# Delta rule's scan: lengths of queries and keys kept as columns, gate sums from two matmuls, decays by subtraction

## The reference, cut to what matters

```python
q_a = l2norm(to_chunks(cq, GDN_HEADS)) * (GDN_HEAD_DIM ** -0.5)
k_a = l2norm(to_chunks(ck, GDN_HEADS))        # x * rsqrt(sum(x*x) + 1e-6)
g_a = -exp(gdn_a_log) * softplus(ga + gdn_dt_bias)
beta_a = sigmoid(gb)

gc = cumsum(g, axis=-1)                                        # inside a chunk
decay = exp(where(incl, gc[..., :, None] - gc[..., None, :], -inf))
kk = einsum('bhnid,bhnjd->bhnij', k, k)
lower = where(strict, beta[..., :, None] * kk * decay, 0.0)
rhs = concatenate([beta[..., None] * v, (beta * exp(gc))[..., None] * k], -1)
sol = triangular_solve(lower, rhs, unit_diagonal=True)         # -> u, w
a_qk = einsum('bhnid,bhnjd->bhnij', q, k) * decay
# for every chunk, in order, with the state S of each head:
delta = u - w @ S
o     = (q * exp(gc)) @ S + a_qk @ delta
S     = exp(gc[-1]) * S + (k * exp(gc[-1] - gc)).T @ delta
# then
o_a = rmsnorm(o, gdn_norm_g) * silu(gz)       # eps 1e-6 inside the mean
```

## Time and profile before

| | |
|---|---|
| median of three runs | 2850.66 us |
| the profiled execution's own time | 2850.46 us |
| its span, first to last instruction | 2849.1 us |
| PE matmul busy | 2665.6 us, 94% |
| DVE busy | 1396.9 us, 49% |
| ACT busy | 913.2 us, 32% |
| POOL busy | 172.9 us, 6% |
| granted TensorE clock, mean | 0.967 of full speed |

### The profile page before, as it was taken

How to read it: one execution, slowest core, us unless ns; L and a number is a source line. 1 busy time by engine, 2 the same in 40 slices (tenths; PEclk the granted TensorE clock), 3 DMA queues, 4 the chain that set the end, 5 groups by cost and what they waited for, 6 DMA issues and landing times.

```text
span 2849.1 us, 34291 instructions
## 1 busy us (share of the span) xinstructions
PE 2665.6 (94%) x15010; PEld 2231.9 (78%) x15010; DVE 1396.9 (49%) x1632; ACT 913.2 (32%) x1254; POOL 172.9 (6%) x185
## 2 busy tenths in 40 slices
PE   6988989989998999999988999889999999999998
PEld 4866778878887877787877987678888878788886
DVE  5664453444365436565355337556553354433333
ACT  4332223244334443122233237532122232322222
POOL 0001230000001000000012100010000100100001
PEclk9998999999999999999999999999999999999999
DMA  3210000221132314454222200035542223232221
GB/s 115 84 64 31 16 17 31 90 75 69 64 133 96 127 59 171 154 207 155 97 82 74 75 30 1 1 135 210 206 158 90 93 85 104 74 104 90 102 94 69
DMA packets 39302, 265.74 MB, mean 93 GB/s; under 512 B 4256, under 2 KB 4640, under 8 KB 8944
## 3 DMA queue, kind: packets, MB, share of 16 engines
q1 hardware_dynamic: 29520, 205.67, 20.9%
q0 software_dynamic: 8256, 55.41, 5.5%
q10 hardware_dynamic: 1376, 2.47, 0.2%
HBM read 261.43 MB, written 2.10 MB: 92 GB/s over the span
## 4 chain that ended last, share of the span: by engine, by line
PE 81%; DVE 11%; ACT 6%; issue 2%; POOL 0%; DMA 0%; DVEq 0%; ACTq 0%
PE bank L142 79%; ACT w_hi L148 2%; DVE w_lo L151 2%; DVE ada_acc L159 1%; ACT tmp L148 1%; DVE tmp L159 1%; PE bank L145 1%; DVE dd L151 1%; DVE v_t L159 1%; ACT da_p L148 1%; DVE heads_t L159 1%; DVE da_stat L162 0%; DVE x_t L159 0%; POOL sq L151 0%; DVE k_t L159 0%
## 5 line engine op out<-in xcount | busy, mean ns | idle before, releaser
L142 PE MATMUL bank<-h_hi,w_hi 128*128 128x512 f32 (+1 forms) x1992 | 810.6, 407 | 33.3 <-DVE h_lo L151 11.8
L142 PE MATMUL bank<-h_lo,w_hi 128*128 128x512 f32 (+1 forms) x1992 | 790.4, 397 | 0.0
L142 PE MATMUL bank<-h_hi,w_lo 128*128 128x512 f32 (+1 forms) x1992 | 789.2, 396 | 0.0
L151 DVE TENSOR_TENSOR w_lo<-w_raw,w_hi 128x2048 fp32r<-128x2048 f32 (+2 forms) x197 | 445.2, 2260 | 345.5 <-ACT w_hi L148 345.5
L142 PEld LDWEIGHTS bank<-h_hi,w_hi 128*128 128x128 f32 (+1 forms) x1992 | 382.3, 192 | 123.0 <-issue 18.3
L148 ACT ACTIVATE w_hi<-w_raw 128x2048 fp32r<-128x2048 f32 (+2 forms) x197 | 370.5, 1881 | 319.9 <-PE bank L142 310.0
L142 PEld LDWEIGHTS bank<-h_hi,w_lo 128*128 128x128 f32 (+1 forms) x1992 | 381.5, 191 | 83.3 <-issue 1.0
L142 PEld LDWEIGHTS bank<-h_lo,w_hi 128*128 128x128 f32 (+1 forms) x1992 | 382.5, 192 | 76.2 <-issue 1.9
L142 PE MATMUL bank<-f_hi,w_hi 128*128 128x512 f32 x672 | 264.5, 394 | 1.1 <-DVE w_lo L151 1.1
L142 PE MATMUL bank<-f_hi,w_lo 128*128 128x512 f32 x672 | 263.6, 392 | 0.0
L142 PE MATMUL bank<-f_lo,w_hi 128*128 128x512 f32 x672 | 263.4, 392 | 0.0
(11 more groups left out here) (336 smaller groups left out, 3333.2 us busy)
## 6 DMA issues: line engine op xcount, KB each, us to landing
w_raw<-in_pack_ffn SPq DMA_DIRECT2D x60, 1024.0 KB, 4.9
ada_w<-in_ada_w POOLq DMA_DIRECT2D x48, 1024.0 KB, 5.3
w_raw<-in_pack_mlp SPq DMA_DIRECT2D x32, 1024.0 KB, 5.1
w_raw<-in_pack_gdn_qkv SPq DMA_DIRECT2D x12, 1024.0 KB, 4.9
w_raw<-in_pack_sc_cu SPq DMA_DIRECT2D x8, 1024.0 KB, 5.0
w_raw<-in_pack_ffn SPq DMA_DIRECT2D x8, 768.0 KB, 4.2
w_raw<-in_pack_gdn_z SPq DMA_DIRECT2D x4, 1024.0 KB, 4.9
w_raw<-in_pack_gate_a SPq DMA_DIRECT2D x4, 1024.0 KB, 5.0
```

Source lines behind the costliest of these rows:

```text
L142: return self.engine.matmul(*a, **k) if self.engine is not None else self
L151: return self.engine.tensor_tensor(*a) if self.engine is not None else self
```

## The change

1. **No spreading of lengths.** `l2_tensor` and `l2_vector` go, with the tensor `l2_inverse`. Queries and keys are not scaled. The keys' squared lengths go into columns: `key_half`, half of the key's length, ahead of the values in the right-hand side, and beta times the inverse squared length, which replaces beta. The queries' length goes into the epsilon of the norm after the scan (`query_eps`).
2. **Gate sums once.** After tile 6 PE does two 128x32 matmuls for all chunks and heads; ACT and DVE make the columns `g_sum`, `from_first` and `to_last`. The scan's step `sums` goes.
3. **Decays by subtraction.** The scan's first step is now `e_row`, four 128x128 matmuls for a group, whose weights are a gate column repeated. DVE subtracts `g_sum` and takes the minimum with a table `least` (0 or -1e30), four 128x128 instructions for a group, into `e_t`; ACT takes the exponential in place. The step `e_t` of PE, DVE's `g_u` and Pool's mask go.
4. **Right-hand side.** In the first chunk the values are scaled on DVE instead of ACT. In the others the 128x512 instruction of DVE becomes four of 128x128, since its scalar is now a column.
5. **The norm after the scan.** DVE makes mean plus `query_eps`, ACT's root follows on it.

```diff
     def conv_tensor(T_, rings):
...
-        T_.background, T_.pace = l2_tensor(T_, rings), 4
+        T_.background, T_.pace = scan_sums_tensor(T_, rings), 4
-    def l2_tensor(T_, rings):
-        for _ in range(L2_FROM + 4):
-            yield
-        for n in range(2 * GDN_H):
-            bank, before = rings.work.take(("l2", n))
...
+    def scan_sums_tensor(T_, rings):
+        for _ in range(GATES_FROM):
+            yield
+        bank, before = rings.work.take("gdn_sums")
+        T_.wait_ge(*freed(before))
+        T_.wait_ge(*at("dve_gates", "g"))
+        T_.matmul(bank[:, 0:8 * NCH], const("incl_t"), g_gdn[:, :], start=True, stop=True)
+        T_.matmul(bank[:, 8 * NCH:16 * NCH], const("ones"), g_gdn[:, :], start=True, stop=True).then_inc(
+            *up("pe_gdn", "sums"))
...
+    def columns_scalar(S):
+        for _ in range(GATES_FROM + 4):
+            yield
...
+        S.activation(g_sum, bank_of("gdn_sums")[:, 0:8 * NCH], ACT.Copy).then_inc(*up("act_gdn", "g_sum"))
+        S.activation(from_first, bank_of("gdn_sums")[:, 0:8 * NCH], ACT.Exp).then_inc(*up("act_gdn", "from_first"))
+        S.wait_ge(*at("dve_gdn", "to_last"))
+        S.activation(to_last, to_last, ACT.Exp).then_inc(*up("act_gdn", "to_last"))
...
+        S.activation(v3(key_half), by_chunk(l2_psum()[:, GDN_H:2 * GDN_H, :]), ACT.Sqrt, bias=param("eps"),
+                     scale=0.25).then_inc(*up("act_conv", "key_half"))
...
-    def l2_vector(V):
...
-            V.scalar_tensor_tensor(qkv(n), qkv(n), P ** -0.5 if n < GDN_H else 1.0, bank_of(("l2", n))[:, :],
-                                   ALU.mult, ALU.mult).then_inc(*up("dve_l2", ("scaled", n), frees=("l2", n)))
+    def columns_vector(V):
...
+        V.tensor_tensor(to_last, bank_of("gdn_sums")[:, 8 * NCH:16 * NCH], g_sum, ALU.subtract).then_inc(
+            *up("dve_gdn", "to_last", frees="gdn_sums"))
...
+        V.wait_ge(*at("act_conv", "key_half"))
+        V.tensor_scalar(query_eps.rearrange("p (n c) -> p n c", c=NCH), l2_psum()[:, 0:GDN_H, :], P * EPS,
+                        4 * P * EPS * EPS, ALU.mult, ALU.add).then_inc(*up("dve_l2", "query_eps"))
+        V.tensor_scalar(v3(key_inv), by_chunk(l2_psum()[:, GDN_H:2 * GDN_H, :]), 4 * EPS, None, ALU.add).then_inc(
+            *up("dve_l2", "key_squares", frees="l2_sums"))
...
+        V.reciprocal(key_inv[:, :], key_inv[:, :]).then_inc(*up("dve_l2", "key_inverse"))
...
+        V.tensor_tensor(beta[:, :], beta[:, :], key_inv[:, :], ALU.mult).then_inc(*up("dve_l2", "beta"))
...
     def scan_tensor(T_, rings, grp):
-            bank = bank_for(c, "sums")
-            T_.matmul(bank[:, 0:8], const("incl_t"), gv[:, c, :], start=True, stop=True)
-            T_.matmul(bank[:, 8:16], const("strict"), gv[:, c, :], start=True, stop=True).then_inc(
-                *up("pe_gdn", (grp, c, "sums")))
-            yield
-            bank = bank_for(c, "e_t")
-            T_.wait_ge(*at("dve_gdn", (grp, c, "g_u")))
-            T_.matmul(bank[:, :], const("strict"), flat(g_u[:, :, :]), start=True, stop=True).then_inc(
-                *up("pe_gdn", (grp, c, "e_t")))
-            yield
             bank = bank_for(c, "e_row")
-            T_.matmul(bank[:, :], const("ones"), flat(g_u[:, :, :]), start=True, stop=True).then_inc(
-                *up("pe_gdn", (grp, c, "e_row")))
+            four(bank, lambda h: gv[:, c, 4 * grp + h:4 * grp + h + 1].to_broadcast([P, P]),
+                 lambda h: const("incl_t")).then_inc(*up("pe_gdn", (grp, c, "e_row")))
...
     def scan_scalar(S, grp):
+            S.wait_ge(*at("dve_gdn", (grp, c, "between")))
+            S.activation(flat(t["e_t"][:, :, :]), flat(t["e_t"][:, :, :]), ACT.Exp).then_inc(
+                *up("act_gdn", (grp, c, "e_t")))
...
     def scan_vector(V, grp):
-            V.tensor_tensor(g_u[:, :, :], mask4("incl_t"), col_of(gv, c), ALU.mult).then_inc(*up("dve_gdn", mark("g_u")))
-            yield
-            yield
+            bank = psum(c, "e_row")
+            for h in range(4):
+                V.scalar_tensor_tensor(e_t[:, h, :], bank4(bank)[:, h, :], col(g_sum, c, h), const("least"), ALU.subtract,
+                                       ALU.min).then_inc(*up("dve_gdn", *([mark("between")] if h == 3 else [])))
...
-                        V.scalar_tensor_tensor(flat(change[:, :, :]), bank[:, :], 0.5, flat(change[:, :, :]), ALU.mult,
-                                               ALU.subtract).then_inc(*up("dve_gdn", mark("rest"), frees=mark("v_turned")))
+                        for h in range(4):
+                            V.scalar_tensor_tensor(change[:, h, :], bank4(bank)[:, h, :], col(key_half, c, h),
+                                                   change[:, h, :], ALU.mult, ALU.subtract).then_inc(
...
     def scan_pool(G, grp):
-            G.tensor_tensor(e_t[:, :, :], e_t[:, :, :], mask4("incl_t"), ALU.mult).then_inc(
-                *up("pool_gdn", (grp, c, "e_incl")))
...
     class GatedNorm:
+                V.scalar_tensor_tensor(gated_inv[:, 0:n], bank_of(("gated", self.name))[:, 0:n], 1.0 / (self.n_tiles * P),
+                                       self.eps_of, ALU.mult, ALU.add).then_inc(
```

More of the change, by code:

```diff
@@ L304, in build_program @@
         for grp in range(2):
-            tiles = {n: sb(st, f"{n}_{grp}", W4) for n in ("g_u", "e_row", "e_t", "tt", "change")}
+            tiles = {n: sb(st, f"{n}_{grp}", W4) for n in ("q_dec", "e_row", "e_t", "tt", "change")}
             tiles |= {n: sb(st, f"{n}_{grp}", [P, 4, HB]) for n in ("low", "corner", "pp")}
@@ L997, in scan_tensor @@
         t = scan_tiles[grp]
-        g_u, e_t, tt, change, corner, pp, dd, off = (
-            t[n] for n in ("g_u", "e_t", "tt", "change", "corner", "pp", "dd", "off"))
-        q_dec, a_t, kdec = g_u, e_t, off[:, :, :, :].rearrange("p a h f -> p (a h f)")
+        q_dec, e_t, tt, change, corner, pp, dd, off = (
+            t[n] for n in ("q_dec", "e_t", "tt", "change", "corner", "pp", "dd", "off"))
+        a_t, kdec = e_t, off[:, :, :, :].rearrange("p a h f -> p (a h f)")
         def bank_for(c, name):
@@ L1152, in scan_scalar @@
                     yield
[L1153 to L1158 removed]
+                    if c > 0:
                         yield
@@ L1231, in scan_vector @@
                     yield
-                    if c > 0:
+                    if c == 0:
+                        bank = psum(c, "v_turned")
+                        V.wait_ge(*at("dve_gdn", mark("corner")))
+                        V.tensor_tensor(change[:, :, :], bank4(bank), col_of(v3(key_half), c), ALU.mult).then_inc(
+                            *up("dve_gdn", mark("rest"), frees=mark("v_turned")))
+                    else:
                         yield
@@ L1288, in scan_pool @@
         hs = heads_of(grp)
-        e_t, low, off = t["e_t"], t["low"], t["off"]
+        low, off = t["low"], t["off"]
         def off_level(c, s):
@@ L1304, in scan_pool @@
         for c in range(NCH):
[L1305 removed]
+            for _ in range(3):
                 yield
             off_level(c, 2)
[L1308 to L1310 removed]
             yield
```

112 lines of the change are left out of this document (48 added, 64 removed).

## The result

The changed kernel takes **2804.18 us** (median of 4 runs, 2802.35 to 2806.17), the kernel before 2850.61 us beside it (4 runs): a ratio of 0.9838, 95% interval 0.9823 to 0.9853. Forecast were 2802.6 us, range 2793.0 to 2813.5. The profiled execution of the changed kernel took 2803.94 us, its span is 2802.6 us.

A forecast was written before the change was run, and what follows sets the result against it. PE, busy 94% of the span, was taken as the bound, so only lost PE work or waits save time. Terms -38.2 + 4.0 + 1.9 + 0.5 - 16.1 = -47.9 from 2850.46 gave 2802.6 us; whole range 2793 to 2813.5.

The forecast's parts named there:

- Terms 1 and 2: End of the convolution: spreading goes, -38.2 us; new PE wait for ACT's bank copy, +4.0, and slow clock behind it, +1.9.
- The rival with no new wait: Convolution's end: ACT frees bank 1 in time, so the new wait is zero; 2796.7 us, chance 0.12.
- Term 3: Small work in the convolution: two PE matmuls cost +0.5 us; ACT's and DVE's column instructions lie in existing waits.
- Term 4: Starts of the scan's four chunks, first row product to second group's `turned`: shorter on DVE's chain, together -19.0 us.
- The rival in which VectorE fills the gap: Scan's chunk starts: DVE gets more instructions, no chunk starts earlier, the scan gives nothing; 2818.7 us, chance 0.06.
- What was given back in the scan: Scan: displaced gemm steps +3.1, cover at its end -1.4, smaller right-hand-side instructions +1.2 us.
- The displaced gemm steps: Scan with 16 steps fewer sheds 4.6 gemm steps, which PE must run later: +3.1 us.
- The cover and the right-hand side: Displaced steps cover scan-end steps with no product beside them, -1.4 us; right-hand side's 128x512 instructions become 128-column ones, +1.2.
- The clock: Scan: rival that the clock falls to 1.2 GHz behind each gap, giving back up to 8 us; 2810.6 us, chance 0.15.
- Behind the scan: After the scan: all as long as before, the epsilon on DVE covered by ACT's table load; 0 us.

The follow-up runs named there:

- e5: The changed kernel itself measured once more, with no edit: 2803.69 us.
- e10: The changed kernel with the right-hand side's four column instructions replaced by one of 128x512, keys' lengths left out there: 2802.79 us.
- e11: The changed kernel with matmuls that nobody reads put in front of PE's waits for `turned` in the chunks: 2804.90 us.
- e4: The changed kernel with the next product's banks taken in the order 2, 0, 1 in place of 0, 1, 2: 2799.99 us.
- e7: The changed kernel with the gate sums' column work one tile later: 2803.48 us.
- e3: The changed kernel with four more unread subtractions on DVE ahead of the four of each group and chunk: 2813.63 us.
- e9: The kernel before with the right-hand side's one 128x512 instruction made four of 128x128, constant 0.5: 2849.77 us.
- e6: The changed kernel with GpSimd's product of queries and row decays moved from the chunk's front to level 16: 2799.30 us.
- e8: The changed kernel with bank order 2, 0, 1, GpSimd's product at level 16 and the column work one tile later: 2792.84 us.
- e12: The changed kernel with new bank order, GpSimd's product at level 16, later column work, and unread matmuls in PE's waits for `turned`: 2793.92 us.
- the two halves: The kernel before with only the lengths as columns, 2821.93 us; the changed kernel with spreading, scaling and the single right-hand-side instruction put back, 2836.82 us.
- e1: The kernel before with only the lengths as columns (spreading gone, right-hand side and norm as in the change): 2821.93 us.

## Why the prediction was right

The time missed by 1.6 us, and that it missed by so little is in part luck: in the profiled executions the scan's start came 1.7 us later than forecast and the scan gave 2.0 us less, and 2.3 us behind the scan, which the sum had at nothing and which the change didn't make, hide most of it. By its terms, in the profiled executions:

**Terms 1 and 2**, -38.2 and +4.0 and +1.9: from 178 us to the scan's start -32.4 measured, -32.3 forecast, and -32.4 again in e5, e10 and e11. The wait was 3.92 us and ended by ACT's `conv_in`, and e4 took it away. The rival with no new wait is refuted.

**Term 3**, +0.5: mis-sized. It is +1.5 (0.80 to 2.30 in VectorE's splits; the same 1.5 in e5). I had counted the matmuls and held that ACT's instructions "lie in the waits that they have in every tile". The place decides: ahead of a split ACT has no slack, and there is a wait of 0.69 us for VectorE between its instructions. e7 shows 0.3 with the same work one tile later. The 0.6 us more in the result's execution stand between 68 and 84 us, ahead of all new instructions; e5 hasn't them.

**Term 4**, the fronts: -19.0 forecast, -19.4 measured. Two errors in it cancel: VectorE's masks take 0.7 us more in each second group, and the rest of the chain is shorter than I had rebuilt it. e3 shows that it is VectorE's chain, with 7.5 of 8.6 us of added subtractions on it. The rival in which VectorE fills the gap is refuted.

**What was given back in the scan** was forecast as +2.9 and is +5.3, so my -16.1 for the scan became -14.1. Two terms of it were too small. These are the four stretches of the rest of the scan before (columns as in the earlier trace rows), and then the first and the third of the changed kernel; its second and fourth are shown with e11:

```profile
261.79:298.91 37.12, 35.93 (x622) 30.86 (x623) 13.47 (x23) 9.21 (x21) 7.22 (x9) 0.95 0.01 3
316.91:356.40 39.49, 39.06 (x655) 34.86 (x655) 15.37 (x28) 7.41 (x18) 5.36 (x7) 0.95 0.01 2
370.89:411.58 40.69, 40.02 (x657) 34.86 (x658) 18.48 (x31) 9.69 (x20) 9.01 (x9) 0.96 0.08 28
426.64:473.43 46.79, 44.19 (x679) 39.55 (x680) 15.47 (x24) 11.62 (x24) 7.19 (x9) 0.97 0.07 24
```

```profile
225.73:262.00 36.27, 36.00 (x623) 31.00 (x623) 13.54 (x23) 8.01 (x19) 5.33 (x7) 0.94 0.01 3
...
325.45:365.61 40.16, 39.49 (x655) 34.78 (x655) 18.22 (x35) 9.21 (x19) 5.30 (x7) 0.96 0.09 28
```

*The displaced gemm steps*, forecast +3.1. 39 gemm matmuls stood in the old fronts and 24 stand in the new, so five steps moved, all into the last stretch (679 matmul records before, 694 after). I had priced them as in a stream of their own, 0.68 us a step. But they stand between the scan's steps, and there one takes 0.89 us from its start to the next scan matmul, at the full clock:

```profile
395.30 0.50 PE L142 MATMUL bank<-h_hi,w_hi 128*128 128x512 f32 x1
395.63 0.39 PE L142 MATMUL bank<-h_lo,w_hi 128*128 128x512 f32 x1
395.87 0.40 PE L142 MATMUL bank<-h_hi,w_lo 128*128 128x512 f32 x1
396.19 0.68 PE L142 MATMUL bank<-pp,dd 64*64 64x64 f32 x16
```

Five of them are 4.4 us, an estimate from these rows.

*The cover and the right-hand side*, forecast -1.4 and +1.2. PE's idle time in these stretches fell from 4.9 to 3.4 us, -1.5. The right-hand side is in this: by e9 and e10 it costs about 0.5 us of waiting, so the cover alone gave some 2.0.

*The clock*, forecast 0. A stretch's length times what its clock lacks of 1 is the most that the clock can have cost it: 6.9 us over the four stretches before, 8.5 in the changed kernel, 7.8 in e5. So the clock takes at most 1.7 us more than before in the result's execution, and 0.9 in e5 (the clock's two digits leave a few tenths open). I gave the scan no clock beyond the old one and kept it as a rival with 0.15 and up to 8 us. The rival is mostly refuted: by these rows the old scan had already been paying most of the 6.4 us that e11 gets back. The first stretch shows it best: the same matmuls, PE busy 35.93 us at 0.95 before and 36.00 at 0.94 after, and 34.32 at 1.00 in e11.

Together these are 4.4 - 1.5 + 1.7 = 4.6 of the 5.3 us, and 3.9 of e5's 4.9; 0.7 to 1.0 us stay open, and more where a slow spell did not cost all that it could. The Trainium skill's rule on gaps ("TensorE: Matmul & The Clock Gate", the loop structure section) speaks of long waits between bursts. The waits in the fronts are shorter, down to 1.2 us with one of 2.3 close behind, and a slow spell followed each pair of them in the changed kernel. It doesn't always: e6 has waits of 1.22 and 1.33 us in its third front and a clock of 1.00 behind them, and so has e8 behind its second.

**Behind the scan**, 0: -2.3 and -2.4 in the two executions of the changed kernel, and -2.1 in e9, which is the kernel before but for one instruction; e3, e8 and e12, which have the changed kernel's work there, are back at about the time before, or above it. It looks like the clock's steps again, and is no gain of the change. It made up for the scan's shortfall in the sum by luck.

**Open** remains how much of the 4.7 us missing between the two halves is systematic. The rest of e1's scan is 4.8 us longer than before with the same steps in its fronts. PE's idle time is 1.4 us of it (6.3 for 4.9), and the clock at most 3.5 (0.92, 0.94, 0.96 and 0.94 in the four stretches); in the first, PE is busy 37.24 us in place of 35.93 with the same 622 matmul records. One profiled execution of each doesn't tell whether it is always so.

## What to carry to other kernels

Work that only held an engine up hid how far the others were behind: when it goes, ask what is late next and which buffer ties it, and move the order of banks with the change (4.2 us here). Small instructions cost nothing only where their engine has slack, so place them behind a tile that waits, not ahead of a split. Work that a shorter front pushes out must be priced by rows of the place where it lands: a gemm step took 0.89 us between the scan's steps and 0.68 in a stream. And before a shortfall is put down to the clock, compare the granted clock of the same stretches before and after; most of what the clock takes may have been paid already.

## What the runs showed of the hardware that I had not expected

- A VectorE instruction with two SBUF inputs took 0.42 us alone and 0.83 and 1.37 behind GpSimd instructions already running, while one with a PSUM input kept its 0.67 us. Moving two GpSimd instructions a chunk out of the way gave 4.9 us.
- In the changed kernel TensorE fell to half its clock behind each of the four fronts, after waits of 1.2 to 3.3 us in pairs, and with the waits filled by unread matmuls the clock stayed at 1.00 through the scan: 6.4 us in 217. With waits of 1.2 to 1.6 and 1.3 us in e6 and e8, one front in each was not followed by a slow spell.
- Executions of the same instructions differ by steps of about 1.6 us; in the one shown at 1310 us PE's busy time and granted clock change and no other engine's busy time does. In a kernel of 2800 us, differences of 2 us in one profile are no evidence for an edit; the fronts, which repeat to 0.02 us, are.
